# Six of nine down pieces by seven block products, with one weight sum made in HBM

## The reference

```python
def swiglu(x, w_gate, w_up, w_down):
    return (jax.nn.silu(x @ w_gate) * (x @ w_up)) @ w_down
# first block (RWKV-7 mix and differential attention, then a squared-relu MLP w_ff1, w_ff2, then a gate),
# then two layers, each:
for layer in range(DEPTH_2):
    x = x + FFN_RES_WEIGHT * swiglu(rms_norm(x, norm_ffn1[layer]), ffn1_w_gate[layer], ffn1_w_up[layer], ffn1_w_down[layer])
    x = x + mixed @ w_out[layer]      # attention
    x = x + FFN_RES_WEIGHT * swiglu(rms_norm(x, norm_ffn2[layer]), ffn2_w_gate[layer], ffn2_w_up[layer], ffn2_w_down[layer])
```

## Time and profile before

| | |
|---|---|
| time, median of 3 runs | 1414.42 us (1414.39 to 1414.59) |
| the profiled execution | 1414.2 us, of which the span of its instructions 1412.4 us |
| PE, DVE, ACT, POOL busy in the span | 1403.6, 1150.0, 818.2, 28.1 us |
| granted TensorE clock over the span | 0.998 |
| HBM traffic | 247.64 MB read, 1.05 MB written |

### The profile page before, as it was taken

The page is one execution under the profiler, slowest core; times in us unless marked ns, Lnnn a source line. Parts: engine busy times, 40 slices in busy tenths (PEclk is TensorE's granted clock), DMA queues, the critical chain, the costliest instruction groups (busy, mean ns, idle before and its releaser), DMA issues.

```text
span 1412.4 us, 22777 instructions
## 1 busy us (share of the span) xinstructions
PE 1403.6 (99%) x9163; PEld 1195.6 (85%) x9163; DVE 1150.0 (81%) x1601; ACT 818.2 (58%) x1110; POOL 28.1 (2%) x93
## 2 busy tenths in 40 slices
PE   8999999999999999999999999999999999999999
PEld 7988778888888888889878888888888887888887
DVE  6876686898878887988867888988889798688797
ACT  6735474565447655555866565555555557665562
POOL 1000000000001100000000000000000000000000
PEclk9999999999999999999999999999999999999999
DMA  9441236455565555455334455545555443355543
GB/s 346 174 150 63 91 120 208 173 185 201 197 220 179 202 186 184 174 209 191 141 119 177 179 196 192 208 178 188 201 179 198 164 177 147 113 201 194 181 177 119
DMA packets 37256, 250.15 MB, mean 177 GB/s; under 512 B 4256, under 2 KB 4384, under 8 KB 8096
## 3 DMA queue, kind: packets, MB, share of 16 engines
q1 hardware_dynamic: 36864, 248.51, 49.2%
q10 hardware_dynamic: 288, 0.19, 0.1%
HBM read 247.64 MB, written 1.05 MB: 176 GB/s over the span
## 4 chain that ended last, share of the span: by engine, by line
PE 98%; DVE 1%; DMA 0%; ACT 0%; issue 0%; SPq 0%; DVEq 0%; ACTq 0%
PE ps L2254 24%; PE ps L2173 16%; PE ps L2175 15%; PE ps L2174 15%; PE ps L2261 13%; PE ps L2426 2%; PE ps L2238 1%; PE ps L2242 1%; PE ps L2244 1%; PE ps L2338 1%; PE ps L2639 1%; PE ps L2619 1%; PE ps L2628 1%; PE ps L2411 0%; PE ps L2563 0%; DMA a<-xtin 0%
## 5 line engine op out<-in xcount | busy, mean ns | idle before, releaser
L3061 DVE TENSOR_TENSOR lo<-raw,hi 128x2048 fp32r<-128x2048 f32 (+1 forms) x230 | 522.4, 2271 | 63.7 <-ACT hi L2682 60.9
L2682 ACT CAST hi<-raw 128x2048 fp32r<-128x2048 f32 (+1 forms) x230 | 436.5, 1899 | 192.6 <-PE ps L2175 123.2
L2254 PE MATMUL ps<-h,hi 128*128 128x512 f32 x1504 | 359.0, 390 | 0.0
L2254 PEld LDWEIGHTS ps<-h,hi 128*128 128x128 f32 x1504 | 276.4, 188 | 52.4
L2173 PE MATMUL ps<-hi,a 128*128 128x512 f32 x516 | 204.6, 397 | 0.0
L2175 PE MATMUL ps<-hi,a 128*128 128x512 f32 x516 | 201.4, 390 | 0.0
L2174 PE MATMUL ps<-lo,a 128*128 128x512 f32 x516 | 201.1, 390 | 0.0
L2261 PEld LDWEIGHTS ps<-h,lo 128*128 128x128 f32 x1504 | 192.2, 190 | 7.8
L2261 PE MATMUL ps<-h,lo 128*128 128x256 f32 x1504 | 194.4, 282 | 0.0
L2886 ACT COPY a<-ps 128x256 f32<-128x256 f32 x208 | 76.3, 372 | 157.1 <-PE ps L2254 84.8
L3029 DVE TENSOR_TENSOR a<-ps,a 128x256 f32<-128x256 f32 x208 | 82.2, 419 | 41.7 <-ACT a L2886 41.6
(11 more groups left out here) (379 smaller groups left out, 1827.8 us busy)
## 6 DMA issues: line engine op xcount, KB each, us to landing
raw<-ws SPq DMA_DIRECT2D x227, 1024.0 KB, 4.8
raw<-ws SPq DMA_DIRECT2D x4, 512.0 KB, 8.0
X<-xin SPq DMA_DIRECT2D x8, 256.0 KB, 7.0
raw<-ws SPq DMA_DIRECT2D x4, 256.0 KB, 5.8
out<-X SPq DMA_DIRECT2D x4, 256.0 KB, 2.1
small<-small SPq DMA_DIRECT2D x1, 992.5 KB, 7.4
const<-const SPq DMA_DIRECT2D x1, 900.0 KB, 7.9
a<-xtin SPq DMA_DIRECT2D x3, 256.0 KB, 5.8
```

What stands on the lines that cost most here:

```text
L2254: t = e.matmul(b2(s["slots"][u]), wh[:, k, 128 * u:128 * u + 128], h2[:, k, :, :], start=k == 0, stop=last)
L2682: e.copy(hi[j % NSPL][:, n], raw[j % NRAW][:, n]).then_inc(hi_ready, 1)
L3061: e.tensor_tensor(lo[j % NSPL][:, n], raw[j % NRAW][:, n], hi[j % NSPL][:, n].bitcast(F), ALU.subtract).then_inc(lo_ready, 1)
```

## The change

1. `SEVENS["a"]` gets a sixth index, 5: D5 of each of the four downs is taken by seven products too. The pieces are now D1, D3, D4, D5, D6, D7. Its mixed activations are made in the gate and up stage like those of the others.
2. The downs get a third set of sums. It lies over the gate and up stage's buffers, so the sums for the second seven piece (D3) wait for that stage's last DVE step.
3. The signs of the scheme change, so that the block which was replaced in `raw` is now a plain sum of two weight blocks, w1 + w0. For the downs' 24 seven pieces this sum is made in HBM ahead of time. GpSimd, behind its first `n_root`, waits for the low part of the fifteenth piece, issues 24 copies of a 128 x 512 block from `ws` to a new HBM tensor `block_sums`, waits for them in four groups, and issues 24 accumulating DMAs that add the other block. Nothing is added to PE, DVE or ACT for it.
4. SP loads such a piece by three DMAs (128 x 512 of `ws`, 128 x 512 of `block_sums`, 128 x 1024 of `ws`) behind one more wait, in place of one DMA of 128 x 2048. `landed` counts them.
5. `w_sums` has three DVE operations in the downs in place of four; the cast of the piece no longer waits for the first of them. For `w_ff2` it keeps four, in another order.
6. `sums_early` is no longer called ahead of the low part of the piece before.
7. `seven_add` has eight DVE operations as before, of which two are now plain additions between bank and buffer.

```diff
-SEVENS = {"a": (1, 3, 4, 6, 7), "s": (3, 5, 7, 9, 11)}
+SEVENS = {"a": (1, 3, 4, 5, 6, 7), "s": (3, 5, 7, 9, 11)}
...
-        by_src = {"a": Sevens(5, (aH, aL), [Arena(14 * 4096), Arena(h_at - arena0)], Arena(17 * 4096), (sgm[0], sgm[1], sgs[0])),
+        by_src = {"a": Sevens(6, (aH, aL), [Arena(14 * 4096), Arena(11 * 4096), Arena(h_at - arena0)], Arena(17 * 4096), (sgm[0], sgm[1], sgs[0])),
...
+        def landed(j):
+
+            return 16 * sum(3 if made(n) else 1 for n in range(j % NRAW, j + 1, NRAW))
...
         def emit_lo(j):
-            if not weaving[0] and j + 1 in sevens and sevens[j + 1][0] == "a" and sevens[j + 1][1]:
-                sums_early(j + 1)
...
-                    e.tensor_tensor(WS[:, 1, :], w[:, 3, :], w[:, 1, :], ALU.subtract)
-                    e.tensor_tensor(w[:, 1, :], w[:, 1, :], w[:, 0, :], ALU.subtract).then_inc(wsum_v.sem, 1)
-                    e.wait_ge(wsum_v.sem, s["own"][0])
-                    e.tensor_tensor(WS[:, 0, :], w[:, 3, :], w[:, 1, :], ALU.subtract).then_inc(wsum_v.sem, 1)
-                    e.wait_ge(wsum_v.sem, s["own"][1])
-                    e.tensor_tensor(WS[:, 2, :], w[:, 2, :], WS[:, 0, :], ALU.subtract).then_inc(wsum_v.sem, 1)
+                    if at_once:
+                        e.tensor_tensor(w[:, 1, :], w[:, 1, :], w[:, 0, :], ALU.add).then_inc(wsum_v.sem, 1)
+                        e.wait_ge(wsum_v.sem, s["own"][0])
+                    t = e.tensor_tensor(WS[:, 0, :], w[:, 3, :], w[:, 1, :], ALU.add)
+                    t.then_inc(wsum_v.sem, 1)
+                    e.wait_ge(wsum_v.sem, s["own"][-2])
+                    e.tensor_tensor(WS[:, 1, :], WS[:, 0, :], w[:, 0, :], ALU.subtract)
+                    e.tensor_tensor(WS[:, 2, :], w[:, 2, :], WS[:, 0, :], ALU.add).then_inc(wsum_v.sem, 1)
...
+                    if s["v"] == 1:
+                        e.wait_ge(lo_ready, 15)
+                        for g in range(4):
+                            for n in range(per_stage * g, per_stage * g + per_stage):
+                                e.dma_start(block_sums[n], ws[made_sums[n]][:, 512:1024]).then_inc(copied_out[g], 16)
+                        for g in range(4):
+                            e.wait_ge(copied_out[g], 16 * per_stage)
+                            for n in range(per_stage * g, per_stage * g + per_stage):
+                                e.dma_start(block_sums[n], ws[made_sums[n]][:, 0:512], accum_op=ALU.add).then_inc(sums_out[g], 16)
...
+                    if made(j + NRAW):
+                        n = made_sums.index(j + NRAW)
+                        e.wait_ge(sums_out[n // per_stage], 16 * per_stage)
+                        e.dma_start(raw[i][:, 0:512], ws[j + NRAW][:, 0:512]).then_inc(raw_in[i], 16)
+                        e.dma_start(raw[i][:, 512:1024], block_sums[n]).then_inc(raw_in[i], 16)
+                        e.dma_start(raw[i][:, 1024:2048], ws[j + NRAW][:, 1024:2048]).then_inc(raw_in[i], 16)
+                    else:
+                        e.dma_start(raw[i][:, :], ws[j + NRAW]).then_inc(raw_in[i], 16)
```

More of the change, by code:

```diff
@@ L238, in program @@
         x_in = [[sem(f"x_in{b}{h}") for h in range(2)] for b in range(2)]
+        copied_out = [sem(f"block_copied{g}") for g in range(4)]
+        sums_out = [sem(f"block_sums_out{g}") for g in range(4)]
         raw_in = [sem(f"raw_in{i}") for i in range(NRAW)]
@@ L511, in sums_of, with made @@
             return by_src[src].sums[unit % len(by_src[src].sums)]
+        def made(j):
+            return j in sevens and sevens[j][0] == "a"
+        def landed(j):
+            return 16 * sum(3 if made(n) else 1 for n in range(j % NRAW, j + 1, NRAW))
         sevens = {}
@@ L517, in program @@
                 sevens[i] = (src, SEVENS[src].index(n // 2))
+        made_sums = [n for n in sorted(sevens) if made(n)]
+        per_stage = len(SEVENS["a"])
+        block_sums = nc.dram_tensor("block_sums", (len(made_sums), 128, 512), F, kind="Internal").ap()
         ta = Arena(0)
@@ L623, in sums_early @@
                 in_h = unit == sets - 1
-                summed[j] = [wsum_v.add() for _ in range(3)]
+                in_gates = src == "a" and unit == 1
+                summed[j] = [wsum_v.add() for _ in range(3 if src == "s" else 2)]
                 emit("w_sums", dve=2.6, j=j, own=summed[j], used=sum(n < j for n in sevens) - min(unit, sets - 1),
-                     after=freed[j - SEVENS[src][unit] - 1] if in_h else None)
+                     after=freed[j - SEVENS[src][unit] - 1] if in_h else (ff_v.sem, ff_v.n) if in_gates else None)
         def split_hi():
@@ L631, in split_hi @@
             sums_early(j)
-            emit("hi", act=1.9, j=j, after=freed.get(j - NSPL), sums=summed[j][0] if j in sevens else None)
+            emit("hi", act=1.9, j=j, after=freed.get(j - NSPL), sums=(wsum_v.sem, summed[j][0]) if j in sevens and not made(j) else None)
             if j in sevens:
@@ L2675, in scalar_program @@
                     j = s["j"]
-                    e.wait_ge(raw_in[j % NRAW], 16 * (j // NRAW + 1))
+                    e.wait_ge(raw_in[j % NRAW], landed(j))
                     if s["after"]:
@@ L2679, in scalar_program @@
                     if s["sums"]:
-                        e.wait_ge(wsum_v.sem, s["sums"])
+                        e.wait_ge(s["sums"][0], s["sums"][1])
                     n = slice(LAST_AT[j] if j < 3 else 0, PIECE)
@@ L3040, in mix @@
                     e.tensor_tensor(z[:, 1, :], a[:, 0, first], a[:, 0, second], ALU.subtract)
-                    e.tensor_tensor(a[:, 0, second], a[:, 0, second], a[:, 1, second], ALU.add).then_inc(mix_v.sem, 1)
+                    e.tensor_tensor(a[:, 0, second], a[:, 0, second], a[:, 1, second], ALU.subtract).then_inc(mix_v.sem, 1)
                     e.wait_ge(mix_v.sem, v[0])
@@ L3044, in mix @@
                     e.wait_ge(mix_v.sem, v[1])
-                    e.tensor_tensor(z[:, 2, :], a[:, 1, first], z[:, 0, :], ALU.subtract).then_inc(mix_v.sem, 1)
+                    e.tensor_tensor(z[:, 2, :], a[:, 1, first], z[:, 0, :], ALU.add).then_inc(mix_v.sem, 1)
             def mix_lo(mix_):
@@ L3073, in vector_program @@
                     w = raw[s["j"] % NRAW][:, :].rearrange("p (q n) -> p q n", q=4)
-                    e.wait_ge(raw_in[s["j"] % NRAW], 16 * (s["j"] // NRAW + 1))
+                    at_once = sevens[s["j"]][0] == "s"
+                    e.wait_ge(raw_in[s["j"] % NRAW], landed(s["j"]))
                     if s["used"]:
```

15 lines of the change are left out of this document (6 added, 9 removed).

## The result

The changed kernel takes 1429.12 us (median of 4, 1425.05 to 1431.17) against 1414.41 (4 runs): ratio 1.0098, 95% interval 1.0085 to 1.0111. It is slower by 14.7 us where I had predicted 2.7 us less, and it lies far outside my range of 1411.2 to 1414.6. Its executions are also spread over 6 us, where those of before lie within 0.2.

The account below looks back on a forecast made before the run. PE was taken to bound the kernel, with 98% of the span. The profiled 1414.2 us less 2.72, all other terms 0, gave 1411.5, or 1411.7 by the median; range 1411.2 to 1414.6 us.

Parts of the forecast that it names:

- Removed from PE: D5 of four downs goes from 24 to 21 matmuls, 12 in all at 0.2267 us: 2.72 us less.
- DVE in a down: DVE takes 5.80 us per seven piece against PE's 4.76; PE never waits, smallest lead 0.6 us at D7's sums.
- the second rival: DVE runs out of lead at D6 and D7, 0.4 us of waiting in each down: 1413.3 us, chance 0.12.
- The sixth mixing and the split loads: At most 1.7 us more DVE work in a gate and up pair, and three DMAs per made piece: nothing on the path.
- GpSimd's 48 DMAs: Between 97.1 us and the second norm at 253.30: done by 198 at 2.1 us each, harmless up to 3.25 us each.
- The Trainium skill's rule: DVE can hold GpSimd's descriptor port: 3.1 us per DMA, 149 us for 48, done at 246, seven us before the norm.
- Beside the loads: The 48 DMAs' 36 us of payload fit in 103 us of idle DMA time: value 0, a price would be 0 to 3 us.
- What would show: Predicted profile: PE 12 rows less, same five waits; last accumulating DMA issued at about 200; a load over 12 us signals late loads.
- my signs of being wrong: Any new PE wait of a us, or a time outside the range.

Follow-up runs that it names:

- e3: Changed kernel with the 48 DMAs issued behind the second norm (about 253 us) instead of behind the fifteenth piece's low part: 1411.89 us, ratio 0.9981.
- e1: Changed kernel without the 48 DMAs; the middle load of a made piece takes the plain block from the weights: 1412.04 us, ratio 0.9982.
- e8: Changed kernel with the 48 DMAs behind the twenty-first piece's low part (about 180 us) instead of the fifteenth's: 1412.04 us, ratio 0.9982.
- e4: Changed kernel with only the 24 plain copies of the 48 DMAs, at the same place, the accumulating ones left out: 1417.02 us.
- e7: Changed kernel with all 48 DMAs from the same place, but GpSimd waits after every two for their landing: 1419.35 us.
- e2: Kernel before the change with the same 48 DMAs added at the same place, nothing reading what they write: 1429.99 us, ratio 1.0109.

## Why the prediction was wrong, step by step

- **Removed from PE, 2.72 us:** right. 12 rows less; e3 against before is 1414.57 - 1411.89 = 2.68 us.
- **DVE in a down:** right, and a little too careful. The three sums start 0.72 and 0.61 us apart and the low part 0.60 behind (1.93 in all), a seven piece takes 5.80, and D5 of PE takes 4.76 (619.81 to 624.57). From DVE's timeline in the first down of the changed kernel (19.7 us later than before; answers to the earlier trace rows):

```profile
617.97 0.68 DVE L3096 TENSOR_TENSOR a<-raw 128x512 f32<-128x512 f32 x1
618.69 0.69 DVE L3099 TENSOR_TENSOR a<-a,raw 128x512 f32<-128x512 f32 x1
619.30 0.68 DVE L3100 TENSOR_TENSOR a<-raw,a 128x512 f32<-128x512 f32 x1
619.90 2.29 DVE L3073 TENSOR_TENSOR lo<-raw,hi 128x2048 fp32r<-128x2048 f32 x1
622.10 1.75 DVE L3104 TENSOR_TENSOR a<-a,a 128x1536 fp32r<-128x1536 f32 x1
623.77 0.69 DVE L3096 TENSOR_TENSOR a<-raw 128x512 f32<-128x512 f32 x1
...
627.91 1.75 DVE L3104 TENSOR_TENSOR a<-a,a 128x1536 fp32r<-128x1536 f32 x1
629.57 4.49 DVE L3073 TENSOR_TENSOR lo<-raw,hi 128x2048 fp32r<-128x2048 f32 x2
```

  D7's sums are ready at 629.57 and PE's first product of them starts at 630.69: 1.1 us of lead, where I had 0.6. The other 0.5 is there from the first sum of D3 on (600.56, where 581.35 + 19.71 is 601.06); D1's shorter sums, which I had named and not added, stand ahead of it. No down has a wait of PE; the second rival didn't come about.
- **The sixth mixing and the split loads, 0:** right. e1 has both. A block of `block_sums` lands in 3.8 us.
- **GpSimd's 48 DMAs, off the path until 3.25 us each:** the conclusion held, the size was off on the safe side. They take 0.53 and 0.84 us to issue and have all landed at about 163 us, not 198. The reason that the changed kernel is slow is not GpSimd at the norm. The Trainium skill's rule that I had weighed ("SBUF — State Buffer", "A bandwidth-pool intuition that's wrong", about 620 ns for such a DMA alone and 3100 beside a DVE copy) has its first figure between the 0.53 and 0.84 us of an issue here. Its second didn't show: 24 plain issues took 12.65 us with DVE busy for 2.4 of them, and 12.68 us in e3 with DVE busy for 11.1. DVE's instructions there are TENSOR_TENSOR and not the copy that the page timed.
- **Beside the loads, "value 0; a price would be 0 to 3 us":** this is the step that failed. It measured 17 us (e1 against the changed kernel). I had asked only which *loads* would come late, and those are slow to be missed: even with a median landing of 8.4 us PE and DVE wait for none. I took 36 us of payload at the loads' rate for room in 103 idle us. But the DMAs come in one pile, and an HBM to HBM byte costs more of the engines than a load's: by part 3 of the page the 12.59 MB took 3.9% of 16 engines for 1429.3 us, 56 us, where I had 36. The engines are full for some 60 us, and in that time the instruction queue is a customer too, and one with little lead: PE stops at the end of a packet if the next one is late, and in the dense stretch it uses one up in 4.0 to 5.8 us. It stood on the page of before, in part 3, with 0.3%, and I passed over it for its size.
- **What would show:** I had named a load over 12 us between 97 and 250 us, a GpSimd that issues its last DMA behind 253, and new waits on DVE in the downs. None came (the longest load took 10.6 us, GpSimd was done at 130.65). The row of 253.30 did move, by 19.7 us, but because PE was late and not GpSimd. Both of my signs of being wrong came: the time, and new waits of PE of a us and more. They are on "issue", which I had read at the start only as 0%.

The version that beats both kernels is e3, the change with one line moved: 1411.89 us, ratio 0.9981 [0.9972, 0.9990]; e8 is equal to it.

What stays open: why the loss differs so much from one execution to the next (e4: 1414.7 to 1419.3, e7: 1414.0 to 1427.1), and why a packet starts late rather than at once, since the profile does not show when it was asked for, nor on which of the 16 engines it waits. Whether the engines themselves or HBM behind them hold it up was not separated. The accumulating DMAs alone at that place were not tried.

## What to carry to other kernels

Background DMAs are not free because the loads can stand them: PE's instructions come over the same DMA engines, in packets of 256, and an engine that uses up a packet faster than the next one comes runs dry. So before you place a pile of transfers, count the matmuls per 10 us of the engine that sets the end, and put the pile where that count is low (here 56, not 190 to 290); in this kernel the denser load traffic there did no harm. If a chain of waits shows "issue" on the bound engine, look at the instruction queue's packets beside the ends of the gaps.

## What I had not expected of the hardware

- Full DMA engines (share 0.92 to 1.10) delay PE's instruction packets. In five runs and the changed kernel each gap of over 0.4 us ends 2.2 to 2.7 us behind the start of a 16 KB packet of that queue, and between the ends of two gaps PE takes 256 instructions or a multiple of it.
- After the gap of 6.13 us the granted clock of a stretch of 5.4 us was 0.62, with matmuls 0.43 us apart, and it was low after the one of 2.37 us; after the others, of 0.7 to 1.9 us, it stayed at 1.00, but in e2 it was low (0.70 from 145 to 155 us) behind gaps of 1.75 and 2.00. In sum the gaps cost up to 0.4 of their length once more (5.5 us beside 13.1).
- Issuing is dear where an engine has other work: 24 copies from HBM to HBM held ACT's queue for 17.4 us and SyncE's for 18.1, 0.73 and 0.76 us each, more than GpSimd's 0.53.
- With two DMAs of 256 KB in flight GpSimd waits 3.4 to 9.1 us for each pair to land, 163 us for the 48.
